# The even layer's maxima, sums and copies in another order, and tile 3's transposes moved in three norms

## The chip, the cores and the metric

The program runs on one core of one Trainium2 chip. The metric is the device time of one execution in microseconds. Three executions of the kernel before gave 1262.24 to 1263.27 us, with a median of 1262.67 us.

The core's engines run their own instruction streams side by side and meet at semaphores: TensorE (PE; matmuls and transposes; PEld are its weight loads), VectorE (DVE), ScalarE (ACT), GpSimd (POOL) and SyncE (SP, which issues the loads). TensorE writes to the eight PSUM banks `ps[:, 0..7]`; a bank can be written again only when an engine has emptied it.

## The reference

Two layers on 512 tokens of width 1024, float32. What the change touches is the even layer and the RMSNorms:

```python
h = rms_norm(x, mix_norm_g[0])
a_q, a_k, a_v, b_q, b_k, b_v = split_cols(h @ w_in, EVEN_WIDTHS)     # 3072 columns
o_a = diff_attention(rope(a_q), rope(a_k), a_v, lam)                 # 4 heads, two 64-wide maps each
o_a = rms_norm(o_a, subln_g) * (1.0 - lam_init)                      # per head, over its 128 values
o_b = dilated_attention(rope(b_q), rope(b_k), b_v)                   # 8 heads of 64
x = x + concat(o_a, o_b) @ w_out
x = x + conv_ffn(rms_norm(x, ffn_norm_g[0]), ...)
# odd layer: the same frame around another mixer
# attention: e = exp(s - max(s)), den = sum(e), o = (e @ v) / den, causal, in blocks of 128 queries
```

## The kernel before

**Precision.** Every large product is made of three fp32r passes: the inputs and the weights are split in a high and a low part (`hT_hi`, `hT_lo`, `w_hi`, `w_lo`), and high x high, high x low and low x high are added up in PSUM.

**Groups.** The even layer's attention goes by eight groups: 0 to 3 are the heads of A (a hardware loop on every engine), 4 to 7 are pairs of B's heads (written out). Each engine runs `attention_ab(kind, g, more)` of its own. A group has eight units k: query block i = k // 2 and map or head m = k % 2, with 128 (i + 1) keys. The chain of a unit goes round the engines: TensorE's scores into bank m (L1485 to L1490), VectorE's maximum (`max_unit`, L905), ScalarE's exponential (`exp_unit`, L501 or L504), in B VectorE's weighting (`weigh_unit`, L911), TensorE's transposes (`turn_probs`, L1456, bank 2 + m), ScalarE's copy (`copy_turned`, L512), TensorE's product with the values (`values`, L1472, bank 6 or 7), and after every second unit VectorE's division (`heads_out`, L917 to L928).

**What fills TensorE between the steps.** While group g runs, TensorE computes the projection of group g + 1 in eight parts (`part`, L1429: 12 matmuls of 384 columns into bank 4 or 5), one at a time between scores and transposes (`NEXT_PART`, `PART_AFTER`). Parts 0 to 3 are over the first half of the inputs and are copied out by ScalarE (`copy_low`, L493); parts 4 to 7 are over the second half and are added to these by VectorE (`add_part`, L880). Part u may start when the part before it in its bank is out: part 5 waits for the copy of part 3, part 7 for the sum of part 5. GpSimd then rotates each token tile (`rope_tile`, L324 to L330), and TensorE transposes the result near the group's end (`turn_qk`, L1419), after which `head_highs` and `head_lows` (ScalarE L486 and L488, VectorE L864 and L867) split queries and keys for the next group. VectorE also splits the low parts of the weights (`split_lo`, L797).

**The sub-norm of A's heads** (`sub_norm`, L1117) is scaled by VectorE in groups 4 to 6, four heads of a token tile at a time. In group 6 TensorE starts to transpose these heads (`early_turn`, L1368) for the output projection.

**The norms inside the trunk** (three of them go this way: before the two MLPs and before the odd layer). VectorE adds the last product to x, ScalarE squares, VectorE scales (`scale_x`, L823, into `xn`, which holds two tiles), TensorE transposes the tile (`turn_xn`, L1257), ScalarE makes the high part (L439) and VectorE the low part (`lows`, L805). The first weight tile after the norm (`first_tile`, L1322) has four blocks of 24 matmuls of 256 columns: token half 0 or 1 times channel half s = 0 or 1. Token tiles 2 and 3 are half 1.

The order of the work is written out by hand on every engine.

Of the kernel before, what the change touches and what calls it, by code (L numbers as in the profile page):

```python
# [54 lines left out]
def trunk_program(nc, x_in, weights, consts, masks, vectors, gains, out):  # L55
# [5 lines left out]
    with ExitStack() as ctx:  # L61
# [311 lines left out]
        def _(sc):  # L373
# [140 lines left out]
            def attention_ab(kind, g, more):  # L514

                for k in range(9):
                    if k == 0 and more:
                        copy_low(g + 1, 1, 5)
                    if k < 8:
                        exp_unit(kind, g, k)  # L520
                    if k >= 1:
                        copy_turned(g, k - 1)
                    if k == 1 and more:
                        copy_low(g + 1, 2, 4)
                    if k == 1 and kind == "B" and more == "first":
                        inverse_root(0, 16)
                    if k == 3 and more:
                        copy_low(g + 1, 3, 5)
                        sc.wait_ge(mm_done, 8 * g + 12)
                        split_hi(0, g + 3, UNIT if more == "last" else IN_COLS)  # L530
                    if k == 4 and not more:
                        split_after(W_OUT0)
                    if k == 7 and more == "last":
                        half_high(1, 4, 0, 0)
                        half_high(2, 5, 0, 1)
                if more == "last":
                    half_high(3, 4, 0, 2)
                    half_high(4, 5, 0, 3)
                elif more:
                    copy_low(g + 2, 0, 4)  # L540
                if more:
                    head_highs(g + 1)
                    sc.wait_ge(mm_done, 8 * g + 16)
                    split_hi(1, g + 3, UNIT if more == "last" else IN_COLS)
# [217 lines left out]
        def _(ve):  # L762
# [175 lines left out]
            def attention_ab(kind, g, more, between={}):  # L938

                for k in range(9):  # L940
                    if k < 8:
                        max_unit(g, k)
                    if k == 8 and more == "last":
                        half_low(1, 4, 0, 0)
                        half_low(2, 5, 0, 1)
                    if k >= 4 and k % 2 == 0:
                        heads_out(kind, g, g, (k - 4) // 2)
                    if 4 <= k <= 7 and more:
                        add_part(g + 1, k)
                    if not more and k in OUT_ADD:  # L950
                        add_early(W_OUT0, OUT_ADD[k])
                    if kind == "B" and k < 8:
                        weigh_unit(g, k)
                    if k == 1:
                        split_lo(2 * g + 3, 1, IN_COLS if more else UNIT)
                    if k == 5 and more:
                        split_lo(2 * g + 4, 0, UNIT if more == "last" else IN_COLS)
                    if k in between:
                        between[k]()
# [2 lines left out]
                    half_low(4, 5, 0, 3)  # L962
                if more:
                    head_lows(g + 1)
                heads_out(kind, g, g, 3)

            def attention_c(h, g):
# [136 lines left out]
            own.link(ve.tensor_tensor(neg_lam[:, :], lam_s[:, 3:4], lam_s[:, 2:3], ALU.subtract))  # L1104
            own.link(ve.tensor_scalar(neg_lam[:, :], neg_lam[:, :], -LAM_INIT, None, ALU.add))
            ve.wait_ge(masks_ready, 1)
            with ve.Fori(0, 4) as g:
                end = own.loop(g, 4, 12)
                attention_ab("A", g, "loop")
                end()  # L1110
            variance(0, 16, 1.0 / 128)

            def sub_norm(t):

                for h in range(4):
                    o = y[:, ds(t, 1), 384 * h:384 * h + 128]
                    ins = ve.scalar_tensor_tensor(o, o, rstd[:, ds(4 * t + h, 1)], sub_gain[:, :].unsqueeze(1),  # L1117
                                                  ALU.mult, ALU.mult)
                ins.then_inc(src_ready, 1)

            between = {4: {3: lambda: refine(0, 16), 6: lambda: sub_norm(0)}, 5: {3: lambda: sub_norm(1), 7: lambda: sub_norm(2)},
                       6: {3: lambda: sub_norm(3)}}
            for g, more in ((4, "first"), (5, "next"), (6, "last"), (7, "")):
                attention_ab("B", g, more, between.get(g, {}))
            late_half(0)
# [120 lines left out]
        def _(pe):  # L1246
# [61 lines left out]
            def first_tile(tile):  # L1308
# [1 line left out]
                slot = tile % 2  # L1310
                pe.wait_ge(w_hi_ready, tile + 1)
                for half, s in ((0, 0), (0, 1), (1, 0), (1, 1)):
                    pe.wait_ge(turn_lo, 8 * turns[0] + 4 * half + 4)
                    if half == 0 and s == 0:
                        products = [(k, m) for m in (0, 2, 1) for k in range(KT)]
                    else:
                        products = [(k, m) for k in range(KT) for m in range(3)]
                    for k, m in products:
                        if half == 0 and s == 0 and (k, m) == (0, 1):
                            pe.wait_ge(w_lo_ready, tile + 1)  # L1320
                        h, w = PASSES[m]
                        ins = pe.matmul(ps[:, s, 256 * half:256 * half + 256],  # L1322
                                        w[:, slot, k * 256 + 128 * s:k * 256 + 128 * s + 128],
# [3 lines left out]
                        ins.then_inc(mm_done, 2)  # L1327
                    elif s == 0:
                        turn_xn(2)
                        turn_xn(3)  # L1330
                turns[0] += 1
                norms[0] += 1

# [590 lines left out]
```

## Time and profile before

| | |
|---|---|
| median of three runs | 1262.67 us |
| the profiled execution's own time | 1264.01 us |
| its span, first to last instruction | 1262.2 us |
| TensorE busy | 1231.8 us (98%) |
| VectorE, ScalarE, GpSimd busy | 501.7, 490.7, 564.0 us |
| granted TensorE clock, mean | 0.999 |
| chain that ended last | TensorE 90%, VectorE 4%, ScalarE 2%, issue 2% |

The profile is of one execution. A busy share is time in which an engine has at least one instruction under way. TensorE's matmuls overlap, so that a matmul is listed with 0.33 us where the next one starts 0.17 us after it; short stops are therefore better read from the start of one matmul to the start of the next. The stretches are: start-up to 41 us, groups 0 to 3 to about 158 us, groups 4 to 7 to 279 us, the first such norm at 296 to 310 us, the MLP to 645 us, the second norm, the odd layer from 684 us, the third norm at 885 to 899 us, the second MLP and the final norm.

### The profile page before, as it was taken

Reading aid. Unit: us, or ns where it says so; the run is one execution under the profiler, and the core shown is the slowest. Engines: PE = TensorE matmul, PEld = TensorE weight load, DVE = VectorE, ACT = ScalarE, POOL = GpSimd, SP = SyncE. Lnnn points to the kernel's source line nnn. Section 1 sums busy time; section 2 is a strip of 40 time slices with the busy share of each in tenths; the row PEclk is TensorE's granted clock in tenths of the full one; section 3 lists DMA queues with packets and bytes.
Section 4 is the critical chain, followed back from the end, with each engine's and each line's share of the span. In section 5 each row is a group of like instructions: output and inputs, shape, how many; then the busy total and the mean of one; then the engine's idle time right before and its main releaser. Section 6 shows DMA issues by size and latency. Waiting matters only on the chain.

```text
span 1262.2 us, 17239 instructions
## 1 busy us (share of the span) xinstructions
PE 1231.8 (98%) x6372; PEld 1056.9 (84%) x6376; DVE 501.7 (40%) x891; ACT 490.7 (39%) x714; POOL 564.0 (45%) x501
## 2 busy tenths in 40 slices
PE   6999999999999999999999999999999999999997
PEld 6999999888888888888888879877888888888886
DVE  6655577755212121132324165633512121132325
ACT  4445544544323222243334254533523232233334
POOL 1244344423444444466644441611444444456662
PEclk9999999999999999999999999999999999999999
DMA  6211111112222222212223211210222222222221
GB/s 261 101 67 66 66 67 68 68 67 86 98 100 100 100 100 97 99 71 100 100 100 109 76 67 68 100 68 34 84 100 100 100 100 100 100 70 98 100 100 67
DMA packets 17037, 114.23 MB, mean 91 GB/s; under 512 B 1888, under 2 KB 2016, under 8 KB 4320
## 3 DMA queue, kind: packets, MB, share of 16 engines
q1 hardware_dynamic: 16416, 111.51, 24.5%
q10 hardware_dynamic: 576, 2.10, 0.6%
q8 instruction: 31, 0.51, 0.2%
q14 instruction: 14, 0.11, 0.0%
HBM read 111.50 MB, written 2.10 MB: 90 GB/s over the span
## 4 chain that ended last, share of the span: by engine, by line
PE 90%; DVE 4%; ACT 2%; issue 2%; DMA 1%; POOL 0%; SPq 0%; DVEq 0%; ACTq 0%
PE ps L1351 37%; PE ps L1591 16%; PE ps L1429 8%; PE ps L1300 6%; PE ps L1396 4%; PE ps L1472 3%; PE ps L1322 2%; PE ps L1704 2%; PE ps L1456 2%; PE ps L1341 2%; PE ps L1684 2%; PE ps L1627 1%; PE ps L1257 1%; PE ps L1419 1%; DMA w_raw<-weights 1%
## 5 line engine op out<-in xcount | busy, mean ns | idle before, releaser
L300 POOL TENSOR_TENSOR w_lo<-w_raw,w_hi 128x512 fp32r<-128x512 f32 (+1 forms) x326 | 457.9, 1435 | 534.2 <-ACT w_hi L379 475.3
L379 ACT ACTIVATE w_hi<-w_raw 128x2048 fp32r<-128x2048 f32 (+1 forms) x95 | 175.3, 1845 | 309.5 <-PE ps L1351 155.3
L1351 PE MATMUL ps<-hT_hi,w_hi 128*128 128x512 f32 x688 | 268.0, 390 | 0.0
L1351 PE MATMUL ps<-hT_lo,w_hi 128*128 128x512 f32 x688 | 267.9, 389 | 0.0
L1351 PE MATMUL ps<-hT_hi,w_lo 128*128 128x512 f32 x688 | 267.9, 389 | 0.0
L1351 PEld LDWEIGHTS ps<-hT_hi,w_hi 128*128 128x128 f32 x688 | 129.2, 188 | 26.9
L1351 PEld LDWEIGHTS ps<-hT_lo,w_hi 128*128 128x128 f32 x688 | 129.2, 188 | 26.7
L1351 PEld LDWEIGHTS ps<-hT_hi,w_lo 128*128 128x128 f32 x688 | 129.2, 188 | 26.5
L1026 DVE TENSOR_TENSOR hT_lo<-region,hT_hi 128x2048 fp32r<-128x2048 f32 (+1 forms) x22 | 58.6, 2670 | 144.3 <-ACT hT_hi L594 144.3
L996 DVE SCALAR_TENSOR_TENSOR qk<-ps,vec,qk 128x511 f32<-128x511 f32 x44 | 33.0, 749 | 202.9 <-ACT qk L568 202.9
L568 ACT ACTIVATE qk<-ps,vec 128x512 f32<-128x512 f32 x44 | 34.3, 780 | 178.4 <-PE ps L1351 166.3
L1591 PE MATMUL ps<-w_hi,hT_hi 128*128 128x512 f32 x256 | 99.7, 390 | 0.0
L1591 PE MATMUL ps<-w_lo,hT_hi 128*128 128x512 f32 x256 | 99.7, 389 | 0.0
L1591 PE MATMUL ps<-w_hi,hT_lo 128*128 128x512 f32 x256 | 99.7, 389 | 0.0
L1006 DVE TENSOR_TENSOR region<-ps,qk 128x512 f32 (+1 forms) x44 | 30.4, 691 | 155.4 <-PE ps L1351 155.4
L324 POOL TENSOR_TENSOR tmp<-region,cst 128x256 f32<-128x256 f32 x30 | 23.8, 792 | 142.1 <-DVE region L880 116.4
L1429 PE MATMUL ps<-w_hi,hT_hi 128*128 128x384 f32 x224 | 80.6, 360 | 1.3 <-ACT region L493 1.0
L1429 PE MATMUL ps<-w_hi,hT_lo 128*128 128x384 f32 x224 | 75.3, 336 | 0.0
L1429 PE MATMUL ps<-w_lo,hT_hi 128*128 128x384 f32 x224 | 74.1, 336 | 0.0
L905 DVE TENSOR_REDUCE neg_max<-ps 128x1 f32<-128x128 f32 (+3 forms) x80 | 39.1, 489 | 50.2 <-PE ps L1490 25.4
L1591 PEld LDWEIGHTS ps<-w_hi,hT_lo 128*128 128x128 f32 x256 | 48.1, 188 | 10.0
L1591 PEld LDWEIGHTS ps<-w_hi,hT_hi 128*128 128x128 f32 x256 | 48.1, 188 | 10.0
(226 smaller groups left out, 2159.1 us busy)
## 6 DMA issues: line engine op xcount, KB each, us to landing
w_raw<-weights SPq DMA_DIRECT2D x99, 1024.0 KB, 4.8
x<-x_in SPq DMA_DIRECT2D x4, 512.0 KB, 9.1
gain<-gains ACTq DMA_DIRECT2D x4, 512.0 KB, 3.5
out<-region SPq DMA_DIRECT2D x4, 512.0 KB, 2.6
w_raw<-weights SPq DMA_DIRECT2D x2, 768.0 KB, 8.3
cst<-consts SPq DMA_DIRECT2D x1, 640.0 KB, 12.2
gain<-gains SPq DMA_DIRECT2D x1, 512.0 KB, 4.3
region<-masks SPq DMA_DIRECT2D x1, 384.0 KB, 12.1
```

The costliest lines, as they stand in the source:

```text
L300: ins = pool.tensor_tensor(w_lo[:, slot, cols], w_raw[:, slot, cols], w_hi[:, slot, cols].bitcast(f32), ALU.subtract)
L379: sc.activation(w_hi[:, slot, 0:used], w_raw[:, slot, 0:used], ACT.Copy).then_inc(w_hi_ready, 1)
L568: sc.activation(qk[:, s, :], ps[:, s, :], ACT.Identity, scale=vec[:, ds(8 * i + (col + 2), 1)], bias=vec[:, ds(8 * i + (col + 3), 1)]).the ...
L905: ve.tensor_reduce(neg_max[:, k:k + 1], ps[:, m, 0:w], AX.X, ALU.max, negate=True).then_inc(max_ready, 1)
L996: own.link(ve.scalar_tensor_tensor(qk[:, s, 1:SEQ], ps[:, s, 0:SEQ - 1], vec[:, ds(8 * i + (col + 1), 1)], qk[:, s, 1:SEQ], ALU.mult, ALU. ...
L1026: ve.tensor_tensor(hT_lo[:, places, :], act[:, ds(kt, count), :], hT_hi[:, places, :].bitcast(f32), ALU.subtract).then_inc(act_lo[l], count)
L1300: ins = pe.matmul(ps[:, bank, :], h[:, k0 + k, t * 128:(t + 1) * 128], w[:, slot, k * 512:(k + 1) * 512], start=first and (k, m) == produc ...
L1351: ins = pe.matmul(bank, w[:, slot, k * pitch + 128 * s:k * pitch + 128 * s + 128], h[:, k:k + 1, :], start=k == 0 and n == 0, stop=k == KT ...
L1396: ins = pe.matmul(ps[:, bank or 4 + f % 2, :], h_[:, place + k, t * 128:(t + 1) * 128], w_[:, (n0 + c) % 2, k * 512:(k + 1) * 512], start= ...
L1429: ins = pe.matmul(ps[:, bank, 0:384], h_[:, 4 * half + k, t * 128:(t + 1) * 128], w_[:, half, k * 384:(k + 1) * 384], start=first and k == ...
L1472: ins = pe.matmul(o, probsT[:, m, b * 128:(b + 1) * 128], v, start=b == 0, stop=b == i)
L1591: ins = pe.matmul(ps[:, 4 * c + t, :], a[:, t * 128:(t + 1) * 128], w[:, slot, u * 512:(u + 1) * 512], start=first and u == units[0] and n ...
```

## The change

It moves instructions on VectorE, ScalarE and TensorE and takes none away; the arithmetic stays.

1. ScalarE, all groups with a next one: `copy_low(g + 1, 3)` goes ahead of `copy_turned(g, 2)`.
2. VectorE, all groups: unit 0's maximum of the next group goes ahead of this group's last `heads_out`.
3. VectorE: the sum of part 4 goes ahead of unit 4's maximum and `heads_out(0)`. The sum of part 7 goes ahead of unit 7's maximum: in A directly, in B already into unit 6, ahead of its weighting.
4. VectorE, groups 4 to 6: the sixteen sub-norm instructions, before in four bursts of four, come one at the end of each unit of groups 5 and 6, with fixed instead of run-time addresses.
5. TensorE, `first_tile`: tile 3's transposes go into the middle of the second block. The third block waits for tile 3's high part alone and takes its low-part products last.

```diff
@@ scalar: attention_ab
+                    if k == 3 and more:
+                        copy_low(g + 1, 3, 5)
                     if k >= 1:
                         copy_turned(g, k - 1)
...
                     if k == 3 and more:
-                        copy_low(g + 1, 3, 5)
                         sc.wait_ge(mm_done, 8 * g + 12)
@@ vector: attention_ab
                 for k in range(9):
-                    if k < 8:
+                    if (k == 4 or k == 7 and kind == "A") and more:
+                        add_part(g + 1, k)
+                    if 1 <= k < 8:
                         max_unit(g, k)
...
                         heads_out(kind, g, g, (k - 4) // 2)
-                    if 4 <= k <= 7 and more:
+                    if k in (5, 6) and more:
                         add_part(g + 1, k)
+                    if k == 6 and kind == "B" and more:
+                        add_part(g + 1, 7)
...
                 if more:
                     head_lows(g + 1)
+                    max_unit(g + 1, 0)
                 heads_out(kind, g, g, 3)
@@ vector: main
+            max_unit(0, 0)
             with ve.Fori(0, 4) as g:
...
-            between = {4: {3: lambda: refine(0, 16), 6: lambda: sub_norm(0)}, 5: {3: lambda: sub_norm(1), 7: lambda: sub_norm(2)},
-                       6: {3: lambda: sub_norm(3)}}
+            def sub_norms(first):
+                return {k: lambda n=first + k: sub_norm(n // 4, n % 4) for k in range(9) if first + k < 16}
+
+            between = {4: {3: lambda: refine(0, 16)}, 5: sub_norms(0), 6: sub_norms(9)}
@@ tensor: first_tile
-                    pe.wait_ge(turn_lo, 8 * turns[0] + 4 * half + 4)
-                    if half == 0 and s == 0:
-                        products = [(k, m) for m in (0, 2, 1) for k in range(KT)]
+                    if half == 0:
+                        pe.wait_ge(turn_lo, 8 * turns[0] + 4)
+                    else:
+                        pe.wait_ge(turn_hi, 8 * turns[0] + 8)
+                    if s == 0:
+                        products = [(k, m) for m in ((0, 1, 2) if half else (0, 2, 1)) for k in range(KT)]
...
+                        if half and s == 0 and (k, m) == (0, 2):
+                            pe.wait_ge(turn_lo, 8 * turns[0] + 8)
+                        if half == 0 and s == 1 and (k, m) == (4, 0):
+                            turn_xn(3)
...
                     elif s == 0:
                         turn_xn(2)
-                        turn_xn(3)
```

The first place is the end of a group of A on VectorE: `L864` to `L867` split the next group's heads, `L917` to `L924` are `heads_out(3)`, `L905` is a maximum. Before, the next group's first maximum comes only behind the loop's branch:

```order
L867 TENSOR_TENSOR k_low<-ps,k_high 128x512
L917 RECIPROCAL rden<-den 128x2
...
L924 SCALAR_TENSOR_TENSOR o_tmp,ss<-region 128x128
L1107 REGISTER_ALU
L1107 COMPARE_AND_BRANCH
L770 TENSOR_SCALAR var<-ss 128x16
L905 TENSOR_REDUCE neg_max<-ps 128x1
L911 SCALAR_TENSOR_TENSOR xn,den<-xn,cst 128x128
```

With the change (line numbers are one to seven higher):

```order
L868 TENSOR_TENSOR k_low<-ps,k_high 128x512
L905 REGISTER_ALU
L906 TENSOR_REDUCE neg_max<-ps 128x1
L918 RECIPROCAL rden<-den 128x2
...
L925 SCALAR_TENSOR_TENSOR o_tmp,ss<-region 128x128
L1114 REGISTER_ALU
L1114 COMPARE_AND_BRANCH
L771 TENSOR_SCALAR var<-ss 128x16
L912 SCALAR_TENSOR_TENSOR xn,den<-xn,cst 128x128
```

The maximum has moved over `heads_out(3)` and the branch; the rows behind the branch are those of group 4.

The second place is VectorE in group 6, from the weight split of unit 5 to the first half-tile split. Before:

```order
L797 TENSOR_TENSOR w_lo<-w_raw,w_hi 128x2048
L905 TENSOR_REDUCE neg_max<-ps 128x1
L917 RECIPROCAL rden<-den 128x2
L928 TENSOR_TENSOR region<-ps,rden 128x128
L880 TENSOR_TENSOR region<-region,ps 128x384
L911 SCALAR_TENSOR_TENSOR xn,den<-xn,cst 128x512
L905 TENSOR_REDUCE neg_max<-ps 128x1
L880 TENSOR_TENSOR region<-region,ps 128x384
L911 SCALAR_TENSOR_TENSOR xn,den<-xn,cst 128x512
L885 TENSOR_TENSOR hT_lo<-ps,hT_hi 128x4x128 x2
```

With the change:

```order
L798 TENSOR_TENSOR w_lo<-w_raw,w_hi 128x2048
L1123 SCALAR_TENSOR_TENSOR region<-region,rstd,sub_gain 128x128
L906 TENSOR_REDUCE neg_max<-ps 128x1
L918 RECIPROCAL rden<-den 128x2
L929 TENSOR_TENSOR region<-ps,rden 128x128
L881 TENSOR_TENSOR region<-region,ps 128x384 x2
L912 SCALAR_TENSOR_TENSOR xn,den<-xn,cst 128x512
L1123 SCALAR_TENSOR_TENSOR region<-region,rstd,sub_gain 128x128
L906 TENSOR_REDUCE neg_max<-ps 128x1
L912 SCALAR_TENSOR_TENSOR xn,den<-xn,cst 128x512
L886 TENSOR_TENSOR hT_lo<-ps,hT_hi 128x4x128 x2
```

The sum of part 7 stands beside that of part 6, ahead of unit 6's weighting, and two sub-norm instructions have come between the split and unit 7's maximum.

The third place is TensorE in `first_tile`. Before:

```order
L1322 MATMUL ps<-hT_hi,w_hi 128x256 x8
L1322 MATMUL ps<-hT_lo,w_hi 128x256 x8
L1322 MATMUL ps<-hT_hi,w_lo 128x256 x8
L1257 MATMUL ps<-cst,xn 128x128 x16
L1322 MATMUL ps<-hT_hi,w_hi 128x256
L1322 MATMUL ps<-hT_hi,w_lo 128x256
```

With the change:

```order
L1337 MATMUL ps<-hT_hi,w_hi 128x256 x8
L1337 MATMUL ps<-hT_lo,w_hi 128x256 x8
L1337 MATMUL ps<-hT_hi,w_lo 128x256 x8
L1265 MATMUL ps<-cst,xn 128x128 x8
L1337 MATMUL ps<-hT_hi,w_hi 128x256
...
L1337 MATMUL ps<-hT_lo,w_hi 128x256
L1265 MATMUL ps<-cst,xn 128x128 x8
L1337 MATMUL ps<-hT_hi,w_hi 128x256
```

The sixteen transposes are now eight and eight, with twelve products between them.

## Rows read from the trace of the kernel before

**Rows 1.** TensorE's waits: for whom, us in total, times, longest us.
```profile
PE ps L1257 <- DVE xn L823: 12.4, 5, 8.0
PE ps L1456 <- ACT xn L504: 1.7, 4, 0.5
...
PE ps L1429 <- ACT region L493: 1.0, 5, 0.2
```

**Rows 2.** Timeline of TensorE in group 2: start us, us, operation, [idle before <-releaser].
```profile
102.32 0.23 PE L1490 MATMUL ps<-mask_bf,ident_bf 128*128 128x128 bf16 x1
102.96 0.33 PE L1456 MATMUL ps<-cst,xn 128*128 128x128 f32 x1 [0.41 <-ACT xn L504]
...
109.18 0.23 PE L1490 MATMUL ps<-mask_bf,ident_bf 128*128 128x128 bf16 x1
109.63 0.45 PE L1429 MATMUL ps<-w_hi,hT_hi 128*128 128x384 f32 x1 [0.21 <-ACT region L493]
...
112.85 0.23 PE L1490 MATMUL ps<-mask_bf,ident_bf 128*128 128x128 bf16 x1
112.89 0.42 PE L1429 MATMUL ps<-w_hi,hT_hi 128*128 128x384 f32 x1
```

**Rows 3.** The same stretch on ScalarE and VectorE.
```profile
102.45 0.37 ACT L504 ACTIVATE xn<-ps,neg_max 128x128 f32<-128x128 f32 x1 [1.62 <-DVE neg_max L905]
...
106.90 0.47 ACT L504 ACTIVATE xn<-ps,neg_max 128x256 f32<-128x256 f32 x1 [0.71 <-DVE neg_max L905]
...
100.15 0.15 DVE L917 RECIPROCAL rden<-den 128x2 f32<-128x2 f32 x1
...
102.12 0.29 DVE L905 TENSOR_REDUCE neg_max<-ps 128x1 f32<-128x128 f32 x1 [0.42 <-DVE o_tmp L924]
```

**Rows 4.** Timeline of TensorE at the start of group 4.
```profile
161.68 0.33 PE L1456 MATMUL ps<-cst,xn 128*128 128x128 f32 x1 [0.51 <-DVE xn L911]
```

**Rows 5.** Timeline at the end of group 4 and in group 5.
```profile
178.22 2.29 DVE L1117 SCALAR_TENSOR_TENSOR region<-region,rstd,sub_gain 128x128 f32<-128x128 f32 x4
...
183.08 0.66 PE L1456 MATMUL ps<-cst,xn 128*128 128x128 f32 x4 [0.67 <-DVE xn L911]
...
196.78 1.13 DVE L1117 SCALAR_TENSOR_TENSOR region<-region,rstd,sub_gain 128x128 f32<-128x128 f32 x4
```

**Rows 6.** Timeline in group 6.
```profile
226.24 0.34 PE L1488 MATMUL ps<-mask_bf,ident_bf 128*128 128x384 bf16 x1
226.68 0.45 PE L1429 MATMUL ps<-w_hi,hT_hi 128*128 128x384 f32 x1
...
235.01 0.68 DVE L905 TENSOR_REDUCE neg_max<-ps 128x1 f32<-128x512 f32 x1
...
238.93 0.63 PE L1368 MATMUL ps<-cst,region 128*128 128x128 f32 x4 [0.90 <-DVE region L880]
...
240.45 0.61 PE L1456 MATMUL ps<-cst,xn 128*128 128x128 f32 x4
```

**Rows 7.** Timeline of norm 1, with norm 3's wait; last the chain.
```profile
307.02 1.03 PE L1257 MATMUL ps<-cst,xn 128*128 128x128 f32 x8
...
307.67 1.28 DVE L823 SCALAR_TENSOR_TENSOR xn<-x,rstd,gain 128x1024 f32<-128x1024 f32 x1
...
309.01 1.09 PE L1257 MATMUL ps<-cst,xn 128*128 128x128 f32 x8 [0.95 <-DVE xn L823]
...
897.65 1.09 PE L1257 MATMUL ps<-cst,xn 128*128 128x128 f32 x8 [1.17 <-DVE xn L823]
...
310.10 8.63 PE ps L1322 x72
```

**Rows 8.** Timeline of GpSimd in group 4, TensorE's weight loads in group 2.
```profile
171.35 0.45 POOL L326 TENSOR_TENSOR tmp<-region,cst 128x128 f32<-128x128 f32 x1
...
174.53 1.97 POOL L326 TENSOR_TENSOR tmp<-region,cst 128x128 f32<-128x128 f32 x1
...
125.69 0.31 PEld L1419 LDWEIGHTS ps<-cst,qk 128*128 128x128 f32 x3 [0.17 <-POOL qk L330]
```

More of the change, by code:

```diff
@@ L1111, in _, with sub_norm @@
             variance(0, 16, 1.0 / 128)
[L1113 to L1119, printed above, removed]
-            between = {4: {3: lambda: refine(0, 16), 6: lambda: sub_norm(0)}, 5: {3: lambda: sub_norm(1), 7: lambda: sub_norm(2)},
-                       6: {3: lambda: sub_norm(3)}}
+            def sub_norm(t, h):
+                o = y[:, t, 384 * h:384 * h + 128]
+                ins = ve.scalar_tensor_tensor(o, o, rstd[:, 4 * t + h:4 * t + h + 1], sub_gain[:, :], ALU.mult, ALU.mult)
+                if h == 3:
+                    ins.then_inc(src_ready, 1)
+            def sub_norms(first):
+                return {k: lambda n=first + k: sub_norm(n // 4, n % 4) for k in range(9) if first + k < 16}
+            between = {4: {3: lambda: refine(0, 16)}, 5: sub_norms(0), 6: sub_norms(9)}
             for g, more in ((4, "first"), (5, "next"), (6, "last"), (7, "")):
```

## The prediction

> **What bounds the kernel now.** I read the page's busy times first: TensorE is at work in 98% of the span, every other engine in less than half of it (the table above). So an edit is worth only what TensorE's stops lose, and 30 us lie outside its busy time, some 15 of them at the start, which the change doesn't touch. Then the waits of TensorE: the largest sum is for `xn`, the scaled token tile of a norm; behind it come the exponential of a unit and the copied part of the projection [rows 1]. That view counts only time in which no matmul is under way, so I measured the short stops in the timeline, from start to start. In group 2 the transposes of unit 0 start 0.64 us after the mask product ahead of them [rows 2], where about 0.06 is the usual step: a stop of 0.6. Part 5 starts 0.45 after its mask product, where the next part's start follows by 0.04 [rows 2]: a stop of 0.4. I looked for the same pattern in all groups. Last came the timeline of the norms, and that of group 6.
>
> **Edit 1, the copy.** Part 5 waits for the copy of part 3, which ScalarE issues behind the copy of unit 2's transposes. That copy waits for TensorE, which made the transposes just before. The exponential of unit 3 is over at 107.4 [rows 3], part 3 has long ended by then, and part 5 isn't wanted before 109.2 [rows 2]. With the copy moved ahead ScalarE has 1.8 us for 0.5 us of work, so the wait goes. It occurs once in each of groups 0 to 6, in group 6 with the same 0.44 from start to start [rows 6]: 7 x 0.42 = 2.9 us. The copy of unit 2's transposes isn't pushed back: it waits for TensorE until after 108 in any case.
>
> **Edit 2, the first maximum.** In group 2 VectorE starts `heads_out(3)` at 100.15 and the maximum of unit 0 at 102.12 [rows 3]. The maximum comes 2 us earlier, which is more than the 0.6 that TensorE waits. ScalarE is busy until about 100.8 and then free, so unit 0's exponential ends by 101.5 against the 102.4 at which TensorE could use it. `heads_out(3)` starts 0.3 us later; nobody waits for its result within this stretch. Groups 1, 2 and 3: 3 x 0.6 = 1.8 us; group 0 has no such stop. In group 4 the stop of some 0.65 us [rows 4] is for the weighted unit 0. The weighting stays behind `heads_out(3)` on VectorE, and only the exponential (0.37, rows 3) leaves the chain: 0.4 us. Groups 5 to 7 have a short `heads_out` and no stop. Sum 2.2 us.
>
> **Edits 3 and 4 in group 4.** TensorE waits 0.67 us by that view, 0.8 from start to start, for unit 7's weighting, behind a VectorE that had 2.29 us of sub-norm to do first [rows 5]. The burst leaves group 4, and the sum of part 7 leaves the place between unit 7's maximum and its weighting. I count 0.8 us gained. Covered by that: the sum of part 7 now waits inside unit 6, with unit 6's weighting behind it, but the part ends about when the sum of part 6 does, and the weighting is wanted only after the next part's 2.1 us.
>
> **Edits 3 and 4 in group 6.** TensorE waits 0.90 for the sum of part 7 before the second `early_turn`, and I count some 0.4 more on the half tiles after it. The sum moves forward, so this wait goes. What is late next is unit 7's chain: the 2048-column weight split holds unit 6's maximum to 235.01 [rows 6], and behind it stand now, ahead of unit 7's maximum, the sum (0.5) and two sub-norm instructions. Four of these took 1.13 us in group 5 and 2.29 in group 4 [rows 5], so two cost 0.6 to 1.1. Unit 7's maximum started at 237.6; I get 238.3 to 238.8, and with maximum, exponential and weighting of 0.7 each TensorE can turn unit 7 at 240.4 to 241.0. It did so at 240.45 [rows 6]. So the wait moves on to this place, nothing to 0.6 us is lost up to there, and the small waits after it give back 0.4 to 0.6. The bounds are a loss of 0.2 and a gain of 1.3 (all of it); I take a gain of 0.3, which is nearer to the slow rows, since GpSimd works beside VectorE here.
>
> In group 5 sub-norms are added before unit 7's weighting as well; by the same durations it ends 0.2 to 0.7 us before TensorE wants it. I take nothing, and 0.3 lost at the worst.
>
> On sub-norm beside GpSimd: the same four instructions took twice as long in one place as in the other [rows 5], and one GpSimd multiplication took 0.45 us and the same one for the next tile, beside the weight split, 1.97 [rows 8]. The Trainium skill (SBUF — State Buffer, Who interferes with whom) says that a VectorE operation with two SBUF inputs and a GpSimd operation that reads SBUF take an exclusive lock, the loser waiting for the whole instruction. By that rule, spreading the sub-norm over sixteen places makes sixteen chances of a block instead of four bursts; the trace agrees as far as the slow rows go. By the rule group 6 gives 0.0 and the sum is 9.7; with sub-norms as quick as in the quick row it gives 0.6, and the sum is 10.3.
>
> **Edit 5, the three norms.** Tile 2's transposes start at 307.02, and eight take 0.87. Tile 3's `xn` is under way from 307.67 to 308.95, and its transposes start at 309.01 [rows 7]: 1.12 us of stop, and they are then spread over 1.09 instead of 0.87, 0.22 more. Now twelve products come first. Seventy-two took 8.63 us [rows 7], so twelve take 1.44: 307.89 + 1.44 = 309.33, later than `xn` is ready. The wait is gone. One more change from transposes to products costs about 0.1 (the first product steps on by 0.20 instead of 0.12). Gain 1.12 + 0.22 - 0.1 = 1.2 us. Norm 2 has the same numbers within 0.02. In norm 3 the idle time is 1.17 against 0.95 [rows 7], so 1.4 us; there `xn` is ready only 0.1 to 0.2 before the twelve products end, still in time. Sum 3.8 us. What is late next is tile 3's high part for block 3: its transposes end 0.1 to 0.3 us later than before, ScalarE needs 1.2 us for two copies, of which the first is hidden, and block 3 starts at 311.8; the second copy is over by 311.1. The low part comes 0.6 later and is wanted only after sixteen products, 1.9 us on. Neither waits.
>
> **The sum.** 2.9 + 2.2 + 0.8 + 0.3 + 3.8 = 10.0 us. Behind each place TensorE runs on in a closed row of products, in the MLP without a stop, and weights and their splits follow its pace, so what is gained is not given back at a later wait. Against the profiled execution's own 1264.0 us that is 1254.0. That execution lies 1.3 above the median of 1262.67; carried over to the median it is 1252.7 us.
>
> **Rivals.**
> *A. GpSimd takes back what the groups gain.* The rotated tile 3 is wanted by `turn_qk`, and there is no slack: in group 2 the last three weight loads already waited 0.17 us for it [rows 8]. A stop that is removed behind the start of the rotation becomes a wait for GpSimd. Against: the stops of edits 1 and 2 lie ahead of part 6, and the rotation of tile 2 starts with the sum of part 6, which moves along with TensorE; only groups 4 and 6 have a stop behind it. If the rotations kept their old times all the same, the 6.2 us of the groups would be lost and the norms' 3.8 left: 1258.9.
> *B. The norms give nothing.* If block 3 waited for ScalarE's copy as long as TensorE stopped before, 6.2 us would be left: 1256.5. For it: ScalarE has a weight split of 1.9 us just ahead of these copies. Against: the split ends at 308.7, before tile 3's transposes.
> *C. The other side, slower: tile 3's rotation falls beside a weight split.* GpSimd's work moves against VectorE's, and a multiplication beside the split took 1.5 us more, 1.97 if it could not have started at all [rows 8]. With no slack at tile 3 this would go to TensorE in all seven groups, 7 x 1.97 = 13.8 us against the 10.0 gained: 1266.5. It decides from 1.4 us a group on. Against: the split is issued in unit 5, and tiles 2 and 3 are rotated in units 7 and 8.
>
> **How the numbers follow.** The forecast 80%, with the bounds of groups 5 and 6 in it (0.8 less or 1.0 more at most). A 5%, B 7%, a mixture of parts of both 4%, no net change 2%, C 2%. The range: 1251.2 (all of group 6's stop, 1.0, and 0.5 for step readings that are short) to 1256.6 (B) holds 8 of 10 and a little more. A measurement of this kernel can tell about 0.2%, 2.5 us, from no change. Faster by more than that are the forecast, A, B and most of the mixture, 95%; within it 3%; slower 2%.
>
> **What would show it.** Right: in the page's waits the rows for the exponential (L504) and the copy (L493) go or fall to one or two; part 5 starts 0.04 us after its mask product in seven groups; in the norms the second set of transposes starts without idle time, twelve products behind the first; TensorE's busy time falls by a few us less than the span. Wrong: a new row `qk` from GpSimd at `turn_qk` (A or C), a wait for `hT_hi` (L439) at the third block (B), a wait for the weighting (L912) above 0.7 us in group 6 (its lower bound). The forecast as a whole is wrong if the gain is under 6 us, or over 12.

## The result, and the profile after

| | median, us | lowest to highest | runs |
|---|---|---|---|
| before | 1262.62 | 1262.24 to 1263.27 | 4 |
| after | 1253.43 | 1252.27 to 1254.21 | 4 |

The ratio is 0.9925, with a 95% interval of 0.9912 to 0.9937: 9.2 us faster, where 10.0 was forecast. The spans of the profiled executions are 1262.2 and 1252.4 us. Of all executions here one was slow, one of e5's ten with 2505.61 us; it is left out of e5's ratio, and without it e5's median is 1260.83 instead of 1260.94.

First the page's waits of TensorE in the changed kernel; TensorE's lines stand 8 to 15 higher than before.

```profile
PE ps L1265 <- DVE xn L824: 9.2, 2, 8.0
PE ps L1470 <- DVE xn L912: 1.2, 1, 1.2
...
PE ps L1470 <- ACT xn L504: 0.5, 1, 0.5
...
PE ps L1433 <- POOL qk L330: 0.2, 1, 0.2
PE ps L1443 <- ACT region L493: 0.2, 1, 0.2
```

Beside [rows 1]: the wait for `xn` of a norm fell from five occasions to two, that for the exponential (L504) from four to one, that for the copied part (L493) from five to one, which stands at 42 us and not ahead of a part 5. The wait for the weighting (L911 before, L912 now) was 1.2 us in two waits, both in group 4 [rows 4, 5], and is now one of 1.2 in group 6. One row is new: GpSimd's `qk` with 0.2.

The timeline of TensorE, in group 2, at the end of group 4 and in groups 5 and 6:

```profile
100.82 0.23 PE L1504 MATMUL ps<-mask_bf,ident_bf 128*128 128x128 bf16 x1
100.88 0.28 PE L1470 MATMUL ps<-cst,xn 128*128 128x128 f32 x1
...
107.06 0.23 PE L1504 MATMUL ps<-mask_bf,ident_bf 128*128 128x128 bf16 x1
107.10 0.42 PE L1443 MATMUL ps<-w_hi,hT_hi 128*128 128x384 f32 x1
...
176.87 0.78 PE L1486 MATMUL ps<-region,xn 128*128 128x64 f32 x6
177.48 0.61 PE L1470 MATMUL ps<-cst,xn 128*128 128x128 f32 x4
...
208.51 0.55 PE L1433 MATMUL ps<-cst,qk 128*128 128x128 f32 x3 [0.18 <-POOL qk L330]
...
231.54 1.04 PE L1382 MATMUL ps<-cst,region 128*128 128x128 f32 x8
232.41 0.60 PE L1470 MATMUL ps<-cst,xn 128*128 128x128 f32 x4
232.85 0.78 PE L1486 MATMUL ps<-region,xn 128*128 128x64 f32 x6
234.88 0.66 PE L1470 MATMUL ps<-cst,xn 128*128 128x128 f32 x4 [1.24 <-DVE xn L912]
```

The first transposes of group 2 follow their mask product by 0.06, part 5 by 0.04 [both in rows 2 before]. Group 4's last stop [rows 5] is gone. In group 6 the eight transposes of `early_turn` now run in one piece, where a 0.90 us wait had split them [rows 6], but the transposes of unit 7 wait 1.24.

Norm 1, on all engines (the products of its first tile follow at L1337):

```profile
301.04 1.04 PE L1265 MATMUL ps<-cst,xn 128*128 128x128 f32 x8
...
301.70 1.28 DVE L824 SCALAR_TENSOR_TENSOR xn<-x,rstd,gain 128x1024 f32<-128x1024 f32 x1
...
301.83 0.36 PE L1337 MATMUL ps<-hT_hi,w_hi 128*128 128x256 f32 x1
...
303.34 1.04 PE L1265 MATMUL ps<-cst,xn 128*128 128x128 f32 x8
303.98 0.60 ACT L439 ACTIVATE hT_hi<-ps 128x512 fp32r<-128x512 f32 x1 [0.32 <-PE ps L1265]
304.11 0.19 PEld L1337 LDWEIGHTS ps<-hT_hi,w_hi 128*128 128x128 f32 x1
304.13 0.36 PE L1337 MATMUL ps<-hT_hi,w_hi 128*128 128x256 f32 x1
```

Beside [rows 7]: the second eight transposes start twelve products after the first, 0.36 us after `xn` is ready, without idle time.

**Where the time went.** Both traces hold the same matmuls in the same count, so each can be paired with its fellow. The lead of the changed kernel over the one before, in us, at a matmul of that place:

| behind | start-up | group 4's first unit | group 4 | group 5's turn_qk | group 6 | norm 1 | norm 2 | norm 3 |
|---|---|---|---|---|---|---|---|---|
| lead | -0.1 | 4.4 | 5.6 | 5.6 | 5.9 | 7.2 | 8.4 | 9.9 |

One by one, as the change of the lead from a few matmuls ahead of a place to a few behind it: the seven stops ahead of part 5 gave 0.43 four times, then 0.37, 0.34 and 0.35, together 2.8. The first units of groups 1 to 4 gave 0.61 to 0.65 three times and 0.47, 2.4. Group 4's end gave 0.88. `turn_qk` gave 0.15 in each of groups 0, 2 and 3, and in group 5 took 0.41. In group 6, behind part 5, 1.09 was gained at `early_turn`, 1.45 lost ahead of unit 7's transposes, 0.41 returned: 0.05. The norms themselves gave 1.2, 1.2 and 1.4; another 0.1 came between the second and the third.

### The profile page after: what moved, and what is told of

The parts are those of the page before. It is cut to its first block, busy times and chain, and to the rows that moved or that the text cites. A ratio compares the mean times of both kernels' runs of the same rounds, so it can differ in the third digit from the quotient of the medians.

```text
span 1252.4 us, 17234 instructions
## 1 busy us (share of the span) xinstructions
PE 1227.9 (98%) x6372; PEld 1056.3 (84%) x6376; DVE 501.7 (40%) x891; ACT 489.2 (39%) x714; POOL 563.9 (45%) x501
## 4 chain that ended last, share of the span: by engine, by line
PE 93%; DVE 3%; ACT 2%; issue 1%; POOL 1%; DMA 1%; SPq 0%; POOLq 0%; DVEq 0%; ACTq 0%
PE ps L1365 37%; PE ps L1605 16%; PE ps L1443 9%; PE ps L1308 6%; PE ps L1410 4%; PE ps L1486 3%; PE ps L1337 3%; PE ps L1718 2%; PE ps L1355 2%; PE ps L1470 2%; PE ps L1698 2%; PE ps L1641 1%; PE ps L1265 1%; PE ps L1499 1%; DMA w_raw<-weights 1%
## 5 line engine op out<-in xcount | busy, mean ns | idle before, releaser
L324 POOL TENSOR_TENSOR tmp<-region,cst 128x256 f32<-128x256 f32 x30 | 29.6, 986 | 136.5 <-DVE region L881 111.0
L1605 PEld LDWEIGHTS ps<-w_lo,hT_hi 128*128 128x128 f32 x256 | 48.0, 188 | 9.9
```

The costliest lines, as they stand in the source:

```text
L1605: ins = pe.matmul(ps[:, 4 * c + t, :], a[:, t * 128:(t + 1) * 128], w[:, slot, u * 512:(u + 1) * 512], start=first and u == units[0] and n ...
```

## The experiments

Two executions of one kernel lay 0.9 us apart at 30 us, in both pairs that were taken, and different kernels with the same code up to there up to 2.3 us (last section), so for each kernel two numbers are given: the median, and its lead behind start-up (lead at the end less lead at 30 us, by paired matmuls). The kernel before had medians of 1263.12, 1262.91 and 1263.10 in the three sets.

**e1: the norms alone**, on the kernel before.

```diff
                     for k, m in products:
+                        if half == 0 and s == 1 and (k, m) == (4, 0):
+                            turn_xn(3)
...
-                        turn_xn(3)
```

> Edit 5 alone, on the kernel before. Theory S (each stop of TensorE that is taken away shortens the run by its own length, and the parts add up): the first matmul behind the norms moves forward by 1.3, 1.2 and 1.5 us as it does in the changed kernel's trace, the span falls by 4.0 us to about 1258.2, and the groups are unchanged. Rival N (the norms' gain is partly the groups' doing, since weights and ScalarE stand earlier there): under 3 us, with a new wait at the third block.

1259.24 (ratio 0.9965, 0.9953 to 0.9978); 3.8 us behind start-up, 1.2, 1.2 and 1.4 at the norms. They give what they give in the whole. Rival B falls.

**e2: the groups alone**, the change without its norms.

> Edits 1 to 4 without edit 5. Theory S: the attention ends 5.9 us earlier than before, the norms' stops of 1.1, 1.1 and 1.3 us are back, the span falls by 5.8 to 6.0 us to about 1256.3; with the norms alone the two gains add up to the 9.8 of the whole change. Rival N: the two gains together miss 9.8 by more than 1 us.

1256.99 (0.9948, 0.9932 to 0.9965); 5.8 us behind start-up. With e1 that makes 9.6 of 10.0. Of the rest 0.3 was lost at unit 6 of group 6, though the orders there are those of the changed kernel; e7 shows why. But for that the two halves add up.

**e5 and e6: edit 1 and edit 2, each alone on the kernel before.**

```diff
+                    if k == 3 and more:
+                        copy_low(g + 1, 3, 5)
                     if k >= 1:
                         copy_turned(g, k - 1)
```

> The kernel before with edit 1 alone: ScalarE copies part 3 of the projection right behind the exponential of unit 3. My theory: the 0.42 us stop ahead of part 5 goes in each of groups 0 to 6 and comes back nowhere: 2.9 us less from the start of group 0 to the end of group 6, so about 1260.2 against 1263.1, less or more by what the start-up does. Rival (GpSimd's rotation keeps its times): turn_qk waits longer and under 1 us is gained, about 1262.5.

1260.94 (0.9981, 0.9971 to 0.9991). All seven stops ahead of part 5 are gone, but the lead is 2.3 and not 2.9: it fell back by 0.15 at `turn_qk` of group 1, by 0.20 at group 4's burst of sub-norms and by 0.07 at `turn_qk` of group 5. So the rival works, at about a tenth of its size.

```diff
                 if more:
                     head_lows(g + 1)
+                    max_unit(g + 1, 0)
                 heads_out(kind, g, g, 3)
```

> The kernel before with edit 2 alone: the maximum of the next group's unit 0 ahead of heads_out(3). By the prediction 2.2 us less (3 x 0.6 and 0.4). By the traces of before and after, read since, 2.4 of the stops and up to 0.4 from shorter waits of turn_qk for the rotation, since everything behind the first unit moves earlier: 2.4 to 2.8, about 1260.5. If the 0.4 belongs to the copy instead, it shows in the other kernel of this call and not in this one. Rival (turn_qk waits instead): under 1 us.

1261.41 (0.9987, 0.9977 to 0.9996), a lead of 2.0, less than the 2.4 to 2.8 expected. The stops gave 0.61, 0.63, 0.59 and 0.46, and `turn_qk` of group 1 took 0.17. The 0.46 that `turn_qk` gave in the changed kernel is in neither. It hangs on VectorE's square in unit 6 (L924), which stands ahead of the sum of part 6, and so ahead of the rotation of tile 2. Here it is in the kernel before, beside GpSimd's rotation, in group 0 and then in group 1:

```profile
59.96 0.58 DVE L924 SCALAR_TENSOR_TENSOR o_tmp<-region 128x128 f32 x1
...
59.94 0.46 POOL L328 TENSOR_TENSOR qk<-tmp 128x128 f32<-128x128 f32 x1
```

```profile
89.27 0.29 DVE L924 SCALAR_TENSOR_TENSOR o_tmp<-region 128x128 f32 x1
...
89.28 0.60 POOL L328 TENSOR_TENSOR qk<-tmp 128x128 f32<-128x128 f32 x1
```

The square took 0.58 in groups 0, 2 and 3 and 0.29 in group 1; in e5 and e6 0.57 to 0.60 in all four, and there `turn_qk` of group 1 is the one that loses. In the changed kernel it took 0.29 in all four: edit 3 lets the sum of part 4 go 2.6 us earlier against TensorE, and GpSimd is all but through with the rotation of tile 1 when the square starts. So the traces put the 0.46 down to edit 3; no run has edit 3 alone.

**e7: the third block's wait for the low part kept**, all else as after.

```diff
-                    if half == 0:
-                        pe.wait_ge(turn_lo, 8 * turns[0] + 4)
-                    else:
-                        pe.wait_ge(turn_hi, 8 * turns[0] + 8)
+                    pe.wait_ge(turn_lo, 8 * turns[0] + 4 * half + 4)
```

> The kernel after, but in the third block of each norm's first tile all products wait for the low part of tile 3, as before the change. My theory: the block starts about 3 us behind tile 3's transposes, and ScalarE's two copies and VectorE's two differences (together some 2.5 us behind them) are over by then, so the new waits for the high part alone are worth at most 0.3 us in each norm: 0 to 0.9 us slower than after, 1252.7 to 1254. Rival: they are what makes the early turn pay, and without them each norm stops for the 0.6 us by which the low part comes later: 1.8 us slower or more.

1254.53 (0.9931, 0.9914 to 0.9948). Against a second execution of the changed kernel (e11) it lost 0.40, 0.41 and 0.38 us in the norms, 1.2 in all, between the two theories. Another 0.3 was lost at unit 6 of group 6, where no instruction differs. It comes from one unit earlier: unit 5's weighting and a multiplication of GpSimd start within 0.01 us of each other. In both executions of the changed kernel the weighting took 0.56 and the multiplication 1.15 (its row stands below, at 225.58 us); in e7 and e2 the weighting took 1.15 and the multiplication 0.74. The weight split behind it was 0.28 shorter there, but what follows started 0.3 later, and with it unit 6's weighting, for which TensorE waits. The wait in the norms stands in the weight loads of the third block:

```profile
303.08 2.70 DVE L806 TENSOR_TENSOR hT_lo<-ps,hT_hi 128x512 fp32r<-128x512 f32 x4 [0.22 <-ACT hT_hi L439]
...
305.83 1.01 PEld L1332 LDWEIGHTS ps<-hT_hi,w_hi 128*128 128x128 f32 x8 [0.34 <-DVE hT_lo L806]
```

VectorE's differences end at 305.78, 2.55 us behind the start of the transposes (303.23), as I had counted. But the block wants them at 305.5, 2.3 behind that start and not 3. Two thirds of edit 5's gain need only the early turn, a third needs the later wait too.

**e4: part 7's sum back in unit 7**, on the changed kernel.

```diff
-                    if (k == 4 or k == 7 and kind == "A") and more:
+                    if k in (4, 7) and more:
...
-                    if k == 6 and kind == "B" and more:
-                        add_part(g + 1, 7)
```

> The changed kernel, but in B the sum of part 7 stays in unit 7, ahead of its maximum, as in A; the sub-norms are those of the change. Theory Q: unit 7's maximum in group 6 has the same work ahead of it, so the stop before unit 7's transposes stays at 1.2 to 1.4 us, and the second early_turn waits 0.3 to 0.5 for the sum, which is hidden in that stop: the span stays within 0.3 of 1252.4. Rival P: with unit 6's weighting earlier, unit 7's chain gains 0.5 and the span falls by 0.5.

1252.87 (0.9917, 0.9901 to 0.9934); behind start-up level with after to 0.02 at the end of group 6. The span came as expected and the stops did not: the `early_turn` stop of 1.1 us is back, where 0.3 to 0.5 was expected, and the one ahead of unit 7 falls from 1.4 to 0.45, where it was to stay. In group 6 the earlier sum of part 7 (edit 3) moves a stop and hardly removes any: unit 5's weighting took 1.14 here, as in e2 and e7, and against these two e4 leads by 0.3, half of it from group 5.

**e3, e8, e10: the sub-norms elsewhere**, in pairs instead of singly.

```diff
-            between = {4: {3: lambda: refine(0, 16)}, 5: sub_norms(0), 6: sub_norms(9)}
+            between = {4: {3: lambda: refine(0, 16)}, 5: pairs(0), 6: pairs(8)}
```

This is e3, with pairs behind units 0 to 3 of both groups; e8 has them behind units 0, 1, 3 and 4 of both, e10 behind units 0, 1, 3, 4 and 8 of group 5 and 0, 1 and 3 of group 6.

> The changed kernel, but the sixteen sub-norm instructions come two at a time at the end of units 0 to 3 of groups 5 and 6, so that none stands between the weight split and unit 7's maximum and none beside GpSimd's rotation. Theory Q (the new stops, 1.4 us before unit 7's transposes in group 6 and 0.35 in turn_qk of group 5, come from the sub-norm instructions of units 5 and 6, which took 0.54 each there): the stop in group 6 falls to 0.3 to 0.6, the one in group 5 goes, the span falls by 1.2 to 1.6 us below the changed kernel's 1252.4, to about 1251. Rival P (the stop comes from the sum of part 7 and the weight split, the sub-norms fit in beside them): under 0.4 us of difference.

> The kernel after, with its 16 sub-norm instructions in pairs behind the weightings of units 0, 1, 3 and 4 of groups 5 and 6 (in e3_subnorm_early: units 0 to 3). My theory: the pair behind unit 2 held unit 3's maximum, with it the exponential and the copy of part 3 behind it on ScalarE, and part 5 stopped 0.33 us in groups 5 and 6 of that kernel; without it both stops go and 0.6 us is gained on e3_subnorm_early from the start of group 5 to the end of group 6; the 0.5 before unit 7's transposes in group 6 stays, since that chain waits for TensorE's own scores. Rival: a pair behind unit 4 delays the maximum of unit 5 or the weight split, and what is won is lost there (0 or slower).

> The kernel after, with its 16 sub-norm instructions in pairs behind units 0, 1, 3, 4 and 8 of group 5 and 0, 1 and 3 of group 6: none before unit 3's maximum, none from unit 4 of group 6 on. My theory: part 5 of groups 5 and 6 starts without a stop (0.33 each in e3_subnorm_early), turn_qk in group 5 doesn't wait; the stop before unit 7's transposes in group 6 is 0.5 or 1.4, according to whether VectorE's weighting or GpSimd's addition begins first, which I can't say beforehand. Behind start-up that is 0.6 us better than e3_subnorm_early or 0.3 worse; against after a gain of 0.3 to 1.2. Rival: what is put behind unit 8 of group 5 delays group 6's first maximum and costs 0.3 or more.

| kernel | median | lead on after, behind start-up | turn_qk, group 5 | part 5, groups 5 and 6 | unit 7, group 6 |
|---|---|---|---|---|---|
| after | 1253.43 | | 0.35 | 0 | 1.4 |
| e3 | 1252.50 | 0.6 | 0 | 0.33 twice | 0.5 |
| e8 | 1252.82 | 0.2 | 0 | 0 | 1.4 |
| e10 | 1251.95 | 1.2 | 0 | 0 | 0.5 |

(The leads are those at the end of group 6; the last three columns are stops, from start to start.) The pair behind unit 2 did hold part 3's copy, as supposed: without it both 0.33 us are gone. In e3 I had expected 1.2 to 1.6 us and got 0.6, between theory and rival: these two stops of 0.33 were not foreseen. But e8, which like e3 has no sub-norm behind the split, kept the long stop at unit 7. So what is put between the split and unit 7's weighting is not the whole cause, and my expectation that e8 gains 0.6 us on e3 was wrong. VectorE and GpSimd in e8, and then in e10:

```profile
232.18 1.12 DVE L912 SCALAR_TENSOR_TENSOR xn<-xn,cst 128x512 f32<-128x512 f32 x1 [0.76 <-ACT xn L501]
...
232.04 0.72 POOL L330 TENSOR_TENSOR qk<-tmp 128x256 f32<-128x256 f32 x1
```

```profile
231.77 0.73 DVE L912 SCALAR_TENSOR_TENSOR xn<-xn,cst 128x512 f32<-128x512 f32 x1 [0.75 <-ACT xn L501]
...
231.90 1.18 POOL L330 TENSOR_TENSOR qk<-tmp 128x256 f32<-128x256 f32 x1
```

In e8 GpSimd's addition began 0.14 before VectorE's weighting, and the weighting took 1.12. In e10 the weighting began 0.13 before the addition, and took 0.73, while the addition took 1.18. Whoever starts second takes 0.4 to 0.5 us longer. With unit 7's weighting TensorE waits for VectorE, so there the order counts. In e10 the addition is the one that pays, and `turn_qk` of group 6 comes 0.2 later for it; that is in the 1.2. Why e8 differs isn't separated: it has a pair behind unit 4 that e3 and e10 lack in group 6 (e3 has it behind unit 2), and unit 5's weighting took 1.13 in it and 0.56 in e3 and e10, after which unit 6's took 1.08 and 0.69.

**e9: a small rotation.** From group 1 on GpSimd rotates 8 of 64 columns; the rotation of the others is left out.

```diff
                 for t in range(NT):
                     pool.wait_ge(rope_ready, 8 * g + 2 * t - 2)
-                    rope_tile(g, t)
+                    rope_tile(g, t, 8)
```

> The kernel after, in which GpSimd rotates, from group 1 on, only 8 of the 64 columns of every head (the other columns keep old values; this part of the computation is left out). Its five instructions a tile fall from 0.45 to 0.73 us each to about 0.1 to 0.2, on the same waits. My theory: the weightings of units 6 and 7 in group 6 took 1.08 instead of 0.7 us, or began late, because VectorE's instruction with two SBUF inputs waits for a GpSimd instruction under way; so the stop ahead of unit 7's transposes falls from 1.24 us to the 0.4 to 0.6 that the chain of maximum, exponential and weighting needs in any case, the wait of turn_qk in group 5 (0.35) goes, and the sub-norms all take about 0.3: 1.0 to 2.0 us less than after from the start of group 0 to the end of group 6. Rival: the chain behind the weight split is late by itself, whatever GpSimd does: the stop stays above 1.0, and only the 0.35 and some tenths at the other turn_qk go.

1251.49 (0.9906, 0.9891 to 0.9921). From start-up to the end of group 6 it leads the changed kernel by 1.4: 0.42 at group 5's `turn_qk`, 0.93 in group 6. The orders on VectorE are those of the changed kernel, the sub-norms included; TensorE's wait at unit 7 is 0.31 instead of 1.24. The three views of it, VectorE, GpSimd, TensorE:

```profile
224.98 2.34 DVE L798 TENSOR_TENSOR w_lo<-w_raw,w_hi 128x2048 fp32r<-128x2048 f32 x1
227.24 0.34 DVE L1123 SCALAR_TENSOR_TENSOR region<-region,rstd,sub_gain 128x128 f32<-128x128 f32 x1
...
229.42 0.69 DVE L912 SCALAR_TENSOR_TENSOR xn<-xn,cst 128x512 f32<-128x512 f32 x1
...
225.13 2.26 POOL L325 TENSOR_TENSOR tmp<-region,cst 128x16 f32<-128x16 f32 x1
...
231.14 0.22 POOL L325 TENSOR_TENSOR tmp<-region,cst 128x16 f32<-128x16 f32 x1
...
232.85 0.66 PE L1470 MATMUL ps<-cst,xn 128*128 128x128 f32 x4 [0.31 <-DVE xn L912]
```

For comparison, the changed kernel's group 6, VectorE and GpSimd:

```profile
226.07 2.81 DVE L798 TENSOR_TENSOR w_lo<-w_raw,w_hi 128x2048 fp32r<-128x2048 f32 x1
228.81 0.54 DVE L1123 SCALAR_TENSOR_TENSOR region<-region,rstd,sub_gain 128x128 f32<-128x128 f32 x1
...
230.26 1.01 DVE L881 TENSOR_TENSOR region<-region,ps 128x384 f32<-128x384 f32 x2
231.19 1.08 DVE L912 SCALAR_TENSOR_TENSOR xn<-xn,cst 128x512 f32<-128x512 f32 x1
...
232.20 0.54 DVE L1123 SCALAR_TENSOR_TENSOR region<-region,rstd,sub_gain 128x128 f32<-128x128 f32 x1
...
225.58 1.15 POOL L324 TENSOR_TENSOR tmp<-region,cst 128x256 f32<-128x256 f32 x1 [0.89 <-DVE region L881]
226.69 2.51 POOL L325 TENSOR_TENSOR tmp<-region,cst 128x128 f32<-128x128 f32 x1
```

The split fell from 2.81 to 2.34 us, the sub-norm from 0.54 to 0.34, the weighting from 1.08 to 0.69. The rival is out.

**e11 and e12: the changed kernel and e3 once more**, beside e10.

> The kernel after, unchanged, beside the kernels of this call: 1253.4 as before, and the order of waits as in its first trace (stop of 1.2 to 1.4 ahead of unit 7's transposes in group 6). If the same kernel shows another length of that stop, its length is a matter of the execution and not of the order of instructions. The tile transposes at 16 to 20 us may step by 0.11 or by 0.21 us, as they did in different executions; with the quick step everything lies 0.6 to 1.5 us earlier.

> e3_subnorm_early once more, timed beside after in one call. Behind start-up its trace was 0.6 us ahead of after, so 0.3 to 0.9 us less here (about 1252.8 against 1253.4), if the gain is the kernel's own; if it was the start-up of that execution, no difference. The stop ahead of unit 7's transposes should be 0.5 again if the order of the two engines is fixed by the program, 1.4 if it is chance.

1253.50 (1252.55 to 1254.40, 5 runs) and 1252.92 (1251.26 to 1253.55, 5 runs), e10 in the same set 1251.95 (1251.49 to 1252.20, 4 runs). Behind start-up, up to the end of group 6, e11 follows the first trace of the changed kernel to 0.03 us, and e12 leads by 0.65 where e3 led by 0.58. The stops at unit 7 are 1.41 and 0.51, as before. So the length of this stop repeats, in two kernels with two executions each. In the changed kernel unit 7's own weighting is not the slow one, it took 0.72 both times; late is what stands ahead of unit 7's maximum, the two sub-norms and unit 6's weighting of 1.08. Not every pair of instructions repeats, though. Unit 5's weighting in group 4, VectorE and GpSimd, in the changed kernel and then in e11, which is the same kernel:

```profile
168.34 1.14 DVE L912 SCALAR_TENSOR_TENSOR xn<-xn,cst 128x384 f32<-128x384 f32 x1 [0.19 <-ACT xn L501]
...
168.34 0.73 POOL L324 TENSOR_TENSOR tmp<-region,cst 128x256 f32<-128x256 f32 x1 [1.41 <-DVE region L881]
```

```profile
167.48 0.56 DVE L912 SCALAR_TENSOR_TENSOR xn<-xn,cst 128x384 f32<-128x384 f32 x1 [0.19 <-ACT xn L501]
...
167.47 1.16 POOL L324 TENSOR_TENSOR tmp<-region,cst 128x256 f32<-128x256 f32 x1 [1.41 <-DVE region L881]
```

Where both start within 0.01 us, either can pay, in one and the same kernel. Here it cost TensorE nothing; in group 6 the same pair cost 0.3 (e2, e7). e8 and e10 have one trace each, so it isn't shown that their starts at unit 7, 0.14 and 0.13 apart, always fall as they did. e10 is the fastest complete kernel here; its ratio to before is 0.9909 (0.9894 to 0.9924). That of the changed kernel in this set is 0.9922 (0.9908 to 0.9935); the two intervals overlap, but e10's slowest execution (1252.20) is quicker than the changed kernel's quickest in this set (1252.55), and the one pair of traces has e10 1.2 us ahead.

## Why the prediction was right

- **Edit 1**, 2.9 forecast, 2.8 measured at its seven stops, 2.3 as a lead when done alone (e5). I had said that nothing comes back; 0.5 came back at `turn_qk` and group 4's burst in that kernel.
- **Edit 2**, 2.2 forecast, 2.4 at its stops (2.0 alone, e6). The first unit of group 4 gave 0.47 instead of 0.4.
- **Group 4**, 0.8 forecast, 0.88 measured.
- **Group 6**, a gain of 0.3 forecast, 0.05 measured, within the bounds of -0.2 to 1.3. The mechanism was as described: the wait for part 7's sum goes, and unit 7's chain is late next. In the times of the kernel before (the lead ahead of this place was 5.9 us) unit 7's maximum came at 238.6 and its transposes at 240.8, inside the 238.3 to 238.8 and 240.4 to 241.0 of the prediction. Up to there 0.36 was lost and behind it 0.41 came back, where 0 to 0.6 and 0.4 to 0.6 stood. What put the chain in the later half: unit 6's weighting, ahead of that maximum, took 1.08 beside GpSimd where it had taken 0.71, and I had applied the slow durations to the sub-norms only. e9 then showed a GpSimd instruction of 16 columns that takes 2.26 us beside the weight split, and 0.22 elsewhere. The rule of the Trainium skill (SBUF — State Buffer, Who interferes with whom), that the loser waits for the whole instruction, agrees with that pair of numbers. By it the prediction had worked out 0.0 for group 6, and that is near what came.
- **Group 5**, nothing forecast, 0.3 at the worst; 0.41 was lost, outside my bounds. I had looked at unit 7's weighting there, and the loss is not at it. The sub-norm behind the weight split holds unit 6's maximum and with it the sum that releases GpSimd's tile 2, which then starts after 0.56 us of idle time; the rotation of tile 3 behind it ends late, and `turn_qk` waits. The rows of GpSimd, first the changed kernel, then e10, where no sub-norm stands at that place:

```profile
200.64 0.74 POOL L330 TENSOR_TENSOR qk<-tmp 128x256 f32<-128x256 f32 x1
201.94 0.74 POOL L324 TENSOR_TENSOR tmp<-region,cst 128x256 f32<-128x256 f32 x1 [0.56 <-DVE region L881]
```

```profile
199.78 0.74 POOL L330 TENSOR_TENSOR qk<-tmp 128x256 f32<-128x256 f32 x1
200.47 0.73 POOL L324 TENSOR_TENSOR tmp<-region,cst 128x256 f32<-128x256 f32 x1
```

  e3 and e8 have no sub-norm at that place and no stop at `turn_qk` either. That is rival A's wait, in one group of seven, from a cause that rival A didn't have: an edit that delays VectorE in front of a sum, not the removal of TensorE's stop.
- **The norms**, 3.8 forecast (1.2, 1.2, 1.4), the same measured in the whole and alone (e1). That neither copy nor low part would hold block 3 was right, but the low part only thanks to its wait being set later (e7: 0.4 us a norm).
- **Not in the sum**: 0.46 from shorter waits of `turn_qk` in groups 0, 2 and 3, which made up for group 5. Here too a VectorE instruction had waited for GpSimd, the square L924 (e6).
- **The signs.** Those of being right all came. Two of those of being wrong came as well: the row `qk` from GpSimd (0.2, group 5), and a wait for the weighting above 0.7 us in group 6 (1.24). The second was ill chosen: TensorE, free of the 1.1 us stop ahead of it, reached the place earlier, and only what the wait has over that stop is lost.
- **The sum**: 10.0 forecast; 10.0 by the lead behind start-up, 9.8 by the spans, 9.2 by the medians. Group 6 was 0.25 short and group 5 lost 0.4; the 0.46 that no term foresaw and some tenths at edit 2 and group 4 made up for it, which is luck of that size. Rivals B and C did not occur. TensorE's busy time fell from 1231.8 to 1227.9, 3.9 us against 9.8 of the span, as stated.

## What to carry to other kernels

Measure short stops from start to start of the same pair of instructions, in every group, since a table of waits leaves out the part that lies under a running matmul: it had 1.0 us for the copied part, and the seven stops of 0.4 us were worth 2.8. Before putting a small instruction on an engine with time to spare, look at what it queues ahead of: behind a long split even one sub-norm of 0.54 us cost TensorE 0.4, whereas in pairs between short units, and not ahead of the maximum that a copy waits for, they made no stop of their own (e10). Where VectorE and GpSimd both work on SBUF, give a late chain the slow durations for every instruction in it, or move the chain; and where instructions of both start within hundredths of a us, count on either outcome.

## What the hardware showed unasked

- **Waiting for the other engine shows as duration.** GpSimd's multiplication of 16 columns took 2.26 us beside a 2.34 us split and 0.22 alone (e9). VectorE's sum with one operand in PSUM (L881, 1.01 for two) was as long with the small rotation as with the full one.
- **The start differs between executions.** TensorE's rows of the first norm, in the changed kernel and then in e12, where the code is the same up to there:

```profile
16.28 1.97 PE L1265 MATMUL ps<-cst,xn 128*128 128x128 f32 x8 [1.27 <-DVE xn L824]
17.90 1.63 PE L1641 MATMUL ps<-w_hi,hT_hi 128*128 128x384 f32 x4
19.33 1.29 PE L1641 MATMUL ps<-w_hi,hT_lo 128*128 128x384 f32 x4
```

```profile
15.27 1.09 PE L1268 MATMUL ps<-cst,xn 128*128 128x128 f32 x8 [1.39 <-DVE xn L824]
16.12 0.94 PE L1644 MATMUL ps<-w_hi,hT_hi 128*128 128x384 f32 x4
16.90 0.85 PE L1644 MATMUL ps<-w_hi,hT_lo 128*128 128x384 f32 x4
```

  In the first, products of 384 columns step on by 0.32 us, the pace of 1.2 GHz, until about 20.3 us, though the granted clock is shown as full; TensorE had stood idle for 1.27 before. In e11, the same kernel, the clock shows it: 0.50 from 16 to 19 us, with the same steps of 0.32, and 0.18 from 19.1 us on. In e12 they step by 0.18, the pace of 2.4 GHz, behind an idle time of 1.39. That makes 2.3 us between two traces at 30 us, in which the earlier arrival of the data has a part as well; why one execution is quick there isn't settled. A difference of 1 us between spans proves nothing here; from 30 us on, paired matmuls of the changed kernel and e11 repeat to 0.03 us up to the norms and to 0.2 at the end, those of e3 and e12 to 0.08 throughout.
